# The opening of a two-layer trunk kernel: the order of its first loads, and two pieces of its work moved

## The reference, cut to what matters

```python
def adaln(c, w, b):
    m = jax.nn.silu(c.astype(F32)) @ w.astype(F32) + b.astype(F32)      # w: 1024 x 3072
    shift, scale, gate = jnp.split(m[:, None, :], 3, axis=-1)
    return shift, scale, gate
...
# layer 0:  hn = rmsnorm(x, g) * (1 + scale) + shift;  h = x + gate * layer(hn)
proj = hn @ w_in.astype(F32)                                            # 1024 x 4096
...
a_bar = jnp.exp(a * dt)                                                 # s5_mixer, 64 groups x 64 states
b_bar = ((a_bar - 1.0) / a)[..., None] * lax.complex(b_re.astype(F32), b_im.astype(F32))
```

## Time and profile before

| | us |
|---|---|
| median of 3 runs | 2992.31 (2987.31 to 2993.15) |
| the profiled execution's own time | 2991.0 |
| its span in the trace | 2989.2 |
| PE busy in the span | 2758.0 (92%) |
| DVE busy | 1586.3 (53%) |
| ACT busy | 1099.1 (37%) |

### The profile page before, as it was taken

How to read it: one execution, slowest core, us unless ns; L and a number is a source line. 1 busy time by engine, 2 the same in 40 slices (tenths; PEclk the granted TensorE clock), 3 DMA queues, 4 the chain that set the end, 5 groups by cost and what they waited for, 6 DMA issues and landing times. The chain is left out here.

```text
span 2989.2 us, 36821 instructions
## 1 busy us (share of the span) xinstructions
PE 2758.0 (92%) x13163; PEld 2190.9 (73%) x13163; DVE 1586.3 (53%) x3227; ACT 1099.1 (37%) x2378; POOL 640.4 (21%) x528
## 2 busy tenths in 40 slices
PE   4799998999999799789998899996899999899999
PEld 2677887888888578678886677775787777667776
DVE  5555771555666466454444666664543331465564
ACT  2611221222222222334432555553522221366664
POOL 0004661544454200032322000000000000033332
PEclk7899999999999999899998899998899999999999
DMA  8215446444545455688886555563322223522221
GB/s 255 95 68 138 149 150 156 137 143 145 147 145 157 130 198 189 234 260 260 281 271 202 147 175 166 164 180 99 130 72 86 79 75 120 166 64 85 86 86 64
DMA packets 468474, 445.07 MB, mean 149 GB/s; under 512 B 157796, under 2 KB 366012, under 8 KB 466876
## 3 DMA queue, kind: packets, MB, share of 16 engines
q1 hardware_dynamic: 364788, 337.20, 38.2%
q10 hardware_dynamic: 103504, 105.51, 10.5%
HBM read 281.50 MB, written 162.70 MB: 149 GB/s over the span
## 5 line engine op out<-in xcount | busy, mean ns | idle before, releaser
L2842 PE MATMUL a_pg<-a_hT,a_whl 128*128 128x512 f32 x640 | 257.0, 402 | 3.4 <-DVE a_whl L878 3.4
L2843 PE MATMUL a_pg<-a_hT,a_whl 128*128 128x512 f32 x640 | 252.0, 394 | 0.0
L2844 PE MATMUL a_pg<-a_hT,a_whl 128*128 128x512 f32 x640 | 251.6, 393 | 0.0
L884 PE MATMUL p_g<-hT,w_hl 128*128 128x512 f32 x512 | 212.8, 416 | 0.0
L830 PE MATMUL pg<-hT,w_hl 128*128 128x512 f32 x512 | 206.2, 403 | 7.1 <-DVE w_hl L878 7.1
L832 PE MATMUL pg<-hT,w_hl 128*128 128x512 f32 x512 | 201.9, 394 | 0.0
L831 PE MATMUL pg<-hT,w_hl 128*128 128x512 f32 x512 | 201.7, 394 | 0.0
L886 PE MATMUL p_g<-hT,w_hl 128*128 128x512 f32 x512 | 200.8, 392 | 0.0
L885 PE MATMUL p_g<-hT,w_hl 128*128 128x512 f32 x512 | 200.3, 391 | 0.0
L2842 PEld LDWEIGHTS a_pg<-a_hT,a_whl 128*128 128x128 f32 x640 | 121.7, 190 | 42.1 <-DVE a_whl L878 11.4
L2844 PEld LDWEIGHTS a_pg<-a_hT,a_whl 128*128 128x128 f32 x640 | 121.7, 190 | 26.4
(11 more groups left out here) (521 smaller groups left out, 6848.8 us busy)
## 6 DMA issues: line engine op xcount, KB each, us to landing
s_wt<-s5w_d SPq DMA_DIRECT2D x64, 354.0 KB
w_raw<-in_ev_w_in SPq DMA_DIRECT2D x32, 512.0 KB, 5.5
s5w_d<-gate_sums SPq DMA_DIRECT2D x32, 512.0 KB, 3.0
vo_d<-e_stage ACTq DMA_DIRECT2D x64, 256.0 KB, 3.9
shared<-h_d SPq DMA_DIRECT2D x28, 512.0 KB, 4.1
arena<-in_ada_w SPq DMA_DIRECT2D x8, 1536.0 KB, 12.1
ada_w<-in_ada_w SPq DMA_DIRECT2D x32, 384.0 KB, 8.2
a_raw<-in_od_w_in SPq DMA_DIRECT2D x40, 256.0 KB, 3.5
```

What stands on the lines that cost most here:

```text
L884: nc.tensor.matmul(out, w(0, k), x(0, k), start=(k == 0), stop=False)
L2842: mm(bank, w[:, 0, k, :], x[:, 0, k, :], start=(k == 0), stop=False)
L2843: mm(bank, w[:, 0, k, :], x[:, 1, k, :], start=False, stop=False)
L2844: last = mm(bank, w[:, 1, k, :], x[:, 0, k, :], start=False, stop=(k == KC - 1))
```

## The change

What it does, in the order of the program:

- `ada_w` is loaded in two pieces: shift and scale (2048 of 3072 columns) of all eight tiles first, the gate's 1024 columns later, behind x.
- Between the two quarters of x the first column block of `w_in` is loaded (`raw`), which `front` loaded at its start before. `raw` and a new `b_scale` are allocated before `startup`.
- B is loaded last, in two DMAs (`btx` only). `front` makes `bty` by two copies within SBUF.
- PE sums shift and scale (banks 0 to 3) and turns them, then the gate (banks 4 and 5). ACT copies the gate's banks after the square root. DVE waits for the gate's column in the middle of the eight scalings of x.
- DVE leaves only the factor of B's tables in `b_scale`; the six multiplications move to `front`, n = 3, between `lo(4)` and `lo(5)`. ACT's negation moves to `front`, behind `hi(2)`.

```diff
-                for k in range(KC // 2):
-                    sp.dma_start(wr[k], wv[0, k]).then_inc(w_in[k], 16)
+                for k in range(KC):
+                    sp.dma_start(wr[k], wv[0, k][:, 0:2 * D]).then_inc(w_in[k], 16)
+                for b in range(2):
+                    sp.dma_start(xring[:, 4 * b:4 * b + 4, :], xv[b]).then_inc(m.x_in[b], 16)
+                    if b == 0:
+                        sp.dma_start(m.raw[:], a["ev_w_in"][0].rearrange("(k p) n -> p k n", p=P)[:, :, 0:P]).then_inc(m.w1_in, 16)
+                for k in range(KC):
+                    sp.dma_start(wg[k], wv[0, k][:, 2 * D:]).then_inc(wg_in, 16)
...
-                sp.dma_start(t.bty[0:NS], bim).then_inc(b_in, 16)
-                sp.dma_start(t.bty[NS:P], bre).then_inc(b_in, 16)
-                for k in range(KC // 2, KC):
-                    sp.dma_start(wr[k], wv[0, k]).then_inc(w_in[k], 16)
-                for b in range(2):
-                    sp.dma_start(xring[:, 4 * b:4 * b + 4, :], xv[b]).then_inc(m.x_in[b], 16)
...
@@ startup, ACT
-                act.wait_ge(b_in, 16 * 4)
-                nc.scalar.mul(t.bty[0:NS], t.bty[0:NS], -1.0).then_inc(b_ready, 1)
                 act.wait_ge(sums_done, 1)
-                for n in range(6):
+                for n in range(4):
...
                 nc.scalar.activation(m.stat[:, 2, 0:2], m.stat[:, 1, 0:2], ACT.Sqrt).then_inc(root_ready, 1)
+                act.wait_ge(sums_done, 2)
+                for n in range(4, 6):
+                    nc.scalar.copy(arow[:, n * 512:(n + 1) * 512], acc[n][:]).then_inc(rows_ready, 1)
...
@@ startup, PE
+                columns(0, 2 * KC)
+                pe.wait_ge(wg_in, 16 * KC)
+                for k in (0, 4):
+                    done = ada_rows(nc, m.cs, wg, acc[4:6], k)
+                done.then_inc(sums_done, 1)
+                columns(2 * KC, 3 * KC)
+                pe.wait_ge(gate_ready, 1)
...
@@ startup, DVE
-                L(tt(s5t[1][:], s5t[1][:], s5t[5][:], ALU.mult))
+                L(tt(m.b_scale[:, 0], s5t[1][:], s5t[5][:], ALU.mult))
...
                 for j in range(8):
+                    if j == 4:
+                        v.wait_ge(sums_turned, 2)
+                        tt(m.ada[:, 0, 2 * KC:], ps_v[:, 3 * P + 2 * KC:3 * P + 3 * KC], m.cols[:, 2 * KC:3 * KC], ALU.add).then_inc(gate_ready, 1)
                     dve.add(ts(xring[:, j], xring[:, j], m.stat[:, 3, j // 4, j % 4:j % 4 + 1], None, ALU.mult))
...
@@ front, SP
-                weights(0)
                 for j in range(4):
                     sp.dma_start(xt[3][j], xv[3, :, j]).then_inc(m.x_in[3], 16)
                 weights(1)
+                sp.wait_ge(m.b_in, 16 * 2)
+                sp.dma_start(t.bty[0:NS], t.btx[NS:P]).then_inc(m.b_in, 16)
+                sp.dma_start(t.bty[NS:P], t.btx[0:NS]).then_inc(m.b_in, 16)
                 sp.wait_ge(turned, KC)
...
@@ front, ACT
                 hi(2)
+                act.wait_ge(m.b_in, 16 * 4)
+                nc.scalar.mul(t.bty[0:NS], t.bty[0:NS], -1.0).then_inc(b_ready, 1)
...
@@ front, DVE: b_tables() waits b_ready and has the six products and sums of before
                     lo(n + 1)
                     if n in (2, 4):
                         circles(n // 4)
+                    if n == 3:
+                        b_tables()
```

More of the change, by code:

```diff
@@ L243, in powers, with ada_rows @@
         n *= 2
-def ada_rows(nc, cs, wr, acc, k, last=False):
-    for n in range(6):
+def ada_rows(nc, cs, wr, acc, k):
+    for n in range(len(acc)):
         for j in range(4):
@@ L269, in startup @@
         rows, crow, crow2 = sb("vec_rows", [P, P]), sb("c_row", [KC, P]), sb("c_row2", [2 * KC, 2, NS])
-        wr = [m.arena[:, k * 3 * D:(k + 1) * 3 * D] for k in range(KC)]
+        wr = [m.arena[:, k * 2 * D:(k + 1) * 2 * D] for k in range(KC)]
+        wg = [m.arena[:, (2 * KC + k) * D:(2 * KC + k + 1) * D] for k in range(KC)]
         arow = sb("ada_rows", [P, 3 * D])
@@ L283, in startup @@
         tw = [work[:, j * G * 8:(j + 1) * G * 8].rearrange("p (g k) -> p g k", k=8) for j in range(4)]
-        s0, s1 = (work[:, j * G * GP:(j + 1) * G * GP].rearrange("p (g k) -> p g k", k=GP) for j in range(2))
         acc = [ctx.enter_context(nc.psum_tensor(f"ps_ada{n}", [P, 512], F32)) for n in range(6)]
@@ L406, in _, with columns @@
                         pe.wait_ge(w_in[k + j], 16)
-                    done = ada_rows(nc, m.cs, wr, acc, k)
+                    done = ada_rows(nc, m.cs, wr, acc[0:4], k)
                 done.then_inc(sums_done, 1)
[L409 to L415, removed]
+                def columns(first, last):
+                    for j in range(first, last):
+                        if j % 4 == 0:
+                            pe.wait_ge(rows_ready, j // 4 + 1)
+                        mm = nc.tensor.matmul(ps_v[:, 3 * P + j:3 * P + j + 1], arow[:, j * P:(j + 1) * P], m.ones[:, 0:1],
+                                              start=True, stop=True, skip_group_check=True)
+                    mm.then_inc(sums_turned, 1)
+                columns(0, 2 * KC)
[5 more added lines that the diff above has]
+                pe.wait_ge(gate_ready, 1)
                 nc.tensor.transpose(ps_v[0:KC, 2 * P:3 * P], m.ada[:, 0, 2 * KC:3 * KC], m.ident[:]).then_inc(gate_turned, 1)
@@ L482, in _ @@
                 L(tt(s5t[2][:], s5t[2][:], s5t[3][:], ALU.subtract))
[L483 to L491, removed]
+                L(tt(m.b_scale[:, 1], s5t[2][:], s5t[5][:], ALU.mult))
                 v.wait_ge(sums_turned, 1)
                 v.wait_ge(cols_ready, 1)
-                L(tt(m.ada[:, 0], ps_v[:, 3 * P:3 * P + 24], m.cols[:, 0:24], ALU.add))
-                v.sem_inc(ada_ready, 1)
+                L(tt(m.ada[:, 0, 0:2 * KC], ps_v[:, 3 * P:3 * P + 2 * KC], m.cols[:, 0:2 * KC], ALU.add))
                 L(stt(out=m.moda[:, 0], in0=m.ada[:, 0, KC:2 * KC], scalar=1.0, in1=m.cols[:, ROWS["norm_g"]:ROWS["norm_g"] + KC],
@@ L528, in front @@
         stage = [sb(f"stage{j}", [P, BT]) for j in range(2)]
-        reg = sb("front_region", [P, 4608])
+        reg = sb("front_region", [P, G * (BW - EBC)])
         f = [reg[:, 2048 + 512 * j:2560 + 512 * j] for j in range(2)]
@@ L550, in front @@
             m.sem(f"n_{n}") for n in "squared mean_ready root_ready scaled turned evacuated hi_done split".split())
-        w_in, w_hi, w_lo = m.sem("p1_w_in"), m.sem("p1_w_hi"), m.sem("p1_w_lo")
+        w_in, w_hi, w_lo = m.w1_in, m.sem("p1_w_hi"), m.sem("p1_w_lo")
+        b_ready = m.sem("s5_b_ready")
         g_done, g_read = m.sem("p1_done"), m.sem("p1_read")
@@ L766, in circles, with b_tables @@
                         v.sem_inc(small_ready, 1)
+                def b_tables():
+                    v.wait_ge(b_ready, 1)
+                    wre, wim = (m.b_scale[:, j].unsqueeze(2).broadcast_to([P, G, GP]) for j in range(2))
+                    s0, s1 = (m.spare[:, j * G * GP:(j + 1) * G * GP].rearrange("p (g k) -> p g k", k=GP) for j in range(2))
+                    L(tt(s0, wim, t.bty[:], ALU.mult))
+                    L(tt(s1, wim, t.btx[:], ALU.mult))
+                    L(tt(t.btx[:], wre, t.btx[:], ALU.mult))
+                    L(tt(t.btx[:], t.btx[:], s0, ALU.add))
+                    L(tt(t.bty[:], wre, t.bty[:], ALU.mult))
+                    L(tt(t.bty[:], t.bty[:], s1, ALU.subtract))
                 def natural(i):
@@ L3175, in trunk @@
             xring = m.arena[:, KC * 3 * D:].rearrange("p (j d) -> p j d", d=D)
+            m.raw = own.enter_context(nc.sbuf_tensor("w_raw", [P, KC, P], F32))
+            m.b_scale = own.enter_context(nc.sbuf_tensor("b_scale", [P, 2, G], F32))
             startup(m, a, tables, xring)
-            m.raw = own.enter_context(nc.sbuf_tensor("w_raw", [P, KC, P], F32))
             m.whl = [own.enter_context(nc.sbuf_tensor(f"w_hl{j}", [P, 2, KC, P], F32R)) for j in range(2)]
```

13 lines of the change are left out of this document (7 added, 6 removed).

## The result

| | before | changed | ratio, 95% interval |
|---|---|---|---|
| first comparison, median (4 and 4 runs) | 2992.73 us (2987.31 to 2994.97) | 2971.16 us (2965.31 to 2976.07) | 0.9927 [0.9915, 0.9938] |
| second comparison, other runs (9 and 5) | 2992.91 us (2991.75 to 2996.03) | 2977.06 us (2974.29 to 2982.48) | 0.9944 [0.9932, 0.9957] |
| profiled executions, span | 2989.2 us | 2968.5 and 2975.2 us | |

Faster by 21.6 us in the first comparison and by 15.9 in the second; 2976.0 was forecast, 16.2 less. The two intervals just overlap, and a part of what follows is on why the same kernel gave two numbers.

A forecast was written before the change was run, and what follows sets the result against it. Bound in the opening by bytes ahead of x and `ada_w`, and a cold weights load after the barrier. 11.9 + 4.3 = 16.2 us off 2992.3 gives 2976 us; range 2969 to 2982, with rivals A and B 2968 to 2985.

The forecast's parts named there:

- The sum's first term: Opening: with B behind the gate's loads, DVE ends at 69.2 instead of 81.09, 11.9 us earlier.
- The landing of 57: Opening: the gate's third of `ada_w` lands at 57 us, bounds 55.5 to 60.
- the sum's 6.0: Opening: PE's 16 gate matmuls, begun cold, take 6.0 us; 3.7 at full clock, 6.8 if never.
- The second term: Start of `front`: first weights already in SBUF, so ACT's high part starts at the barrier; 4.3 us, bounds 2 and 4.4.
- That the gain arrives whole: Behind `front`: a chain through barriers, nothing tied to the program's start, so all 16.2 us should reach the end.
- The tables in `front` at no cost: `front`, n = 3: six DVE operations, 7.5 us, fit where DVE idled 8.93 us; cost 0.
- A (smaller pieces slower): Opening loads: smaller pieces move more slowly, gate lands 7.8 us later; gain 8.4, 2984 us; chance 0.11.
- The 7 us "of the gain": Opening loads: a skill page's rates give `ada_w` and x 49 us against the rows' 42, about 7 us.
- B (tables don't fit): `front`, n = 3: slower table operations take 15.7 us, 6.8 over the gap; 2983 us; chance 0.08.
- C (copies within SBUF late): `front`: late `bty` copies delay ACT, costing one for one beyond 94 us; 3001 us at 125; chance 0.02.
- D (full clock and an earlier landing, 2972): Opening: PE at full clock and data 1.5 us sooner, gain 20; chance 0.74 together with the forecast.
- The four bounds of the forecast: Spread around the total: landing (+1.5, -3), clock (+2.3, -0.8), start of `front` (+0.1, -4), medians some 2.5 us.

The follow-up runs named there:

- e4: Changed kernel with all four of B's loads from HBM at the end and no copies within SBUF; 2975.98 us.
- e6: Changed kernel with the first two products of B's tables made three times, 5.0 us more DVE work; PE's wait 5.86 us instead of 3.35, no total given.
- e8: Changed kernel with block 6's weights loaded ahead of the small tables' store on SP; 2977.9 us.
- e2: Changed kernel with the first column block of `w_in` loaded in `front` again; 2977.34 us.
- e10: Changed kernel unaltered, timed again in five rounds on one chip; 2977.06 us, ratio to before 0.9944.
- e3: Changed kernel with the modulation whole again (full rows of `ada_w`, one sum, then x); 2976.13 us, ratio to before 0.9948.
- e5: Changed kernel with the gate's addition behind all eight scalings of x; 2976.65 us.
- e1: Changed kernel with B's two loads issued before x instead of last; 2983.76 us.
- e7: Changed kernel with the gate's addition behind all eight scalings and the gate summed in two halves as they land; 2974.32 us.

## Why the prediction was right, and where its terms were off

**The sum's first term, 11.9 us.** The mechanism held in its steps. The profiled run showed 14.1: the landing 0.7 us sooner, the sum 5.10 instead of 6.0, the columns at full clock 1.95 instead of 2.4, 0.2 in smaller steps. Over the five runs whose program is the same up to this point, but for e4's loads behind the gate (the changed kernel twice, e4, e6, e8), the gate landed at 56.33, 56.86, 57.35, 56.71 and 56.60, PE summed for 5.10, 6.51, 5.74, 6.42 and 5.19, and the first high part came at 67.24, 69.17, 68.91, 68.94 and 67.59: 68.4 in the mean. The forecast's DVE end of 69.2 is 69.5 in these terms, 1.1 us late in the mean and 2.2 against the run first seen. The landing of 57 was right to 0.2 us; the sum's 6.0 lies within its spread, with a mean of 5.8. From the end of PE's sum to the high part it is 5.8 us in all five. So the size of this term is set by the landing, which moved by 1.0 us, and by the clock that PE gets after its wait, which moved the sum by 1.4. That the landing came out at 57 is in part luck: the full rate ended 9.6 us earlier than before (53.3 against 62.9), where the forecast had the landing 8.3 earlier, and the tail behind it, which the forecast did not have as a term, was 3.0 us long instead of 2.1.

**The second term, 4.3 us,** measured 4.37 in the profile (85.75 - 81.38 before, nothing after). e2 put the load back: 4.2 us behind the barrier, less 1.9 for the bytes in front of the gate, which the forecast had charged with 1.7.

**That the gain arrives whole** is not what the traces show. Of the 18.5 us at the first high part 20.7 are there at the end of the first profile; of e10's 16.6 there are 14.0. Nothing in the program is tied to its start, but which waits are followed by a stretch at 1.2 GHz differs between executions, and that moves the end by 2 to 3 us either way. The forecast had this spread (2.5 us) in its range and not in its argument. It is a likely part of why the first comparison gave 21.6 and the second 15.9: over the nine executions of the changed kernel the time falls with the mean granted clock, from 2982.48 us at 0.961 to 2965.31 at 0.968, though not strictly (2970.26 and 2974.29 both at 0.965). In the two profiles the same ACT instruction is 1.9 us later in e10 at the first high part, 2.8 at 101 us, 5.4 at 158 (behind the stretch shown above) and at the end of the program 6.8. But e4 kept the clock from 140 to 160 us and took 2975.98, so this stretch is only one of several, and the others were not followed up. What decides the clock in one execution is left open, and so is what the chip contributes.

**The tables in `front` at no cost:** right, with less room than forecast. The forecast's 8.93 is DVE's idle time in one execution, between one low part and the end of the next high part. In the changed kernel's profile the same measure is 8.55 - 1.14 = 7.4 us, and in e10's 10.0; the mean clock from 140 to 160 us was 1.00 and 0.83, and in the trace before it was 0.66 from 165 to 170. The six operations of 1.26 us need 7.5, so they cost 0.1 us in one execution and nothing in the other. e6 shows that beyond the cover the price reaches PE.

**The rivals.** A (smaller pieces slower): not seen, 388 to 414 GB/s. The 7 us "of the gain" that the prediction worked out for a lower rate would not have been the gain's: `ada_w` and x have the same bytes in both kernels. B (tables don't fit): not seen, but for 0.1 us; the operations kept 1.23 us, with POOL idle as the earlier trace rows had it. The Trainium skill, SBUF — State Buffer, section SBUF: two separate sides, has a DVE operation with two SBUF inputs contend for a shared port pair only with a GpSimd operation that reads SBUF. The traces agree: 1.23 us here with POOL idle, and in e8 1.42 to 1.78 us beside POOL for operations that take 0.69 us without it, the factor of about two that B had feared. C (copies within SBUF late): they were issued at 70.0 and 71.5 and landed 9.3 and 9.4 us later, at 80.9 at the latest. ACT came to the negation that needs them at 145.16, 64 us later. The prediction's limit of 94 us does not follow from its rows: the 17 us of slack start at `hi(3)` (167.92 before), not at the issue of the copies. And by its own limit a landing at 125 us gives 2976 + 31 = 3007, not 3001. D (full clock and an earlier landing, 2972): the first comparison comes near to this case, with the landing 0.7 us early and the clock full from 60 us on.

**The range.** The four bounds of the forecast added up give 2969 on the fast side, as stated, but 2986 on the slow side, where 2982 was stated; the result lay inside either.

**Margins in `front`'s start:** the second weights were due within 1 to 2 us by the forecast; they were late by 0.27 us in the changed kernel, 0.39 in e3, and not in e4 and e5, nor in the repetition e10.

**SP's queue.** The forecast had SP perhaps stuck on B's second load, at no cost. It was, for 13.84 us, and besides for 14.62 us on x's second quarter, which the forecast had not reckoned with. The DMA engines did not run dry meanwhile. The weights in runs of 512 bytes ahead of it are not the reason: in e2, without them, SP was held as well, on another load, and issued B's first load at 40.06 us, 41.74 in the changed kernel. SP's line in e2:

```profile
19.66 8.89 SPq L328 DMA_DIRECT2D arena<-in_ada_w  x1
```

## What to carry to other kernels

In an opening bound by bytes, list the loads by who waits for them last, and put those with short runs and a late reader behind all others: here 1 MB in runs of 64 bytes held the engines for 10 us at a quarter of their rate, and halving and moving it is, by e1 to e3, the larger part of the gain. Once that is done, a finer split of the last wait (e5, e7) wins 1 to 4 us at the barrier that no total here shows; PE's clock after each wait moves the time by as much. Before work is moved onto DVE or started earlier there, look at what POOL does at that time (e8). Run the same kernel twice before explaining a difference of 5 us, and compare the points of the program where the two traces part.

## What the runs showed of the hardware

- The same wait of 3.43 us in the same program was followed by full clock in one execution and by a stretch at 1.2 GHz in another, 2.5 us apart. The sum of 32 matmuls after a wait of 11.6 to 14.4 us took from 5.10 to 6.51 us.
- The issue of one DMA can hold SP for 14.62 us with the engines at 388 to 414 GB/s; in e2, with no short runs queued, one issue held it for 8.89 us.
- While runs of 64 bytes moved, the rate was 96 GB/s over 10 us before, 105 from 58 to 60 us in the changed kernel, and 99 to 100 from 36 to 40 us in e1: the same in the middle of the queue and at its end.
- Copies of 0.26 MB within SBUF landed 5.5 to 9.8 us after issue, beside other loads (e2 the shortest, e3 the longest).
- DVE operations with two SBUF inputs of 128x512 took 0.68 to 0.69 us with POOL waiting and 1.42 to 1.78 us with POOL at work (changed kernel and e8).
